# Step sizes of the state-space layer in fp32 from x, four 32-column groups at once, and three small halves made by GpSimd

## The reference

```python
hn = rmsnorm(x, norm_mix_pre[0])                 # x * r(token) * g(feature)
proj = einsum('bsd,de->bse', hn, w_in)           # 1024 -> 2*2048 + 2*8*128 + 32
z, xBC, dt = split(proj, ...)
xBC = silu(causal_dwconv(xBC, conv_w, conv_b))
dt = softplus(dt + dt_bias)                      # 32 step sizes a token, one a head
A_cs = cumsum(dt * A) in chunks of 128 tokens    # decays, used by all 8 groups
```

## Time and profile before

| | |
|---|---|
| median of 3 runs | 1422.06 us (1421.97 to 1422.57) |
| profiled execution, its time | 1422.02 us |
| its span in the trace | 1420.2 us |
| TensorE busy | 1405.7 us, 99% of the span |
| VectorE busy | 1003.5 us, 71% |
| ScalarE busy | 623.9 us, 44% |
| GpSimd busy | 112.3 us, 8% |

### The profile page before, as it was taken

One profiled execution on the slowest core, in us unless ns is written; L12 is line 12 of the kernel. 1 busy time (PEld: TensorE's weight loads), 2 busy tenths in 40 slices (PEclk: granted clock), 3 DMA queues, 4 the chain that ended last, 5 costly groups with the idle time before them and its releaser, 6 DMA issues.

```text
span 1420.2 us, 21794 instructions
## 1 busy us (share of the span) xinstructions
PE 1405.7 (99%) x7550; PEld 1184.2 (83%) x7550; DVE 1003.5 (71%) x1510; ACT 623.9 (44%) x1068; POOL 112.3 (8%) x84
## 2 busy tenths in 40 slices
PE   8999999999999999999999999999999999999997
PEld 7888888888889888888888977778798888888887
DVE  6988888889437888888622676768488888887123
ACT  6666556557344323232322446566653322333221
POOL 0000000000110000000011023232110000000111
PEclk9999999999999999999999999999999999999999
DMA  4443333332231222323324112121312323233331
GB/s 175 171 144 124 144 123 114 135 143 77 90 134 34 101 97 95 102 90 108 108 91 145 38 55 81 60 74 59 112 37 89 104 89 103 90 108 102 102 102 60
DMA packets 37445, 142.34 MB, mean 100 GB/s; under 512 B 4176, under 2 KB 6352, under 8 KB 35344
## 3 DMA queue, kind: packets, MB, share of 16 engines
q1 hardware_dynamic: 37392, 141.63, 29.0%
HBM read 139.38 MB, written 2.23 MB: 100 GB/s over the span
## 4 chain that ended last, share of the span: by engine, by line
PE 94%; DVE 3%; issue 1%; DMA 1%; ACT 1%; SPq 0%; POOL 0%; POOLq 0%; ACTq 0%
PE bank L471 21%; PE bank L473 20%; PE bank L472 20%; PE b_x L471 7%; PE b_x L473 7%; PE b_x L472 7%; PE b_norm L1652 1%; PE b_y L1073 1%; PE b_y L471 1%; PE b_y L472 1%; PE b_y L473 1%; DVE hn_lo L815 1%; PE b_x L1085 1%; PE b_y L1076 1%; DVE mbuf L820 1%
## 5 line engine op out<-in xcount | busy, mean ns | idle before, releaser
L419 ACT ACTIVATE w_hi<-raw 128x1024 fp32r<-128x1024 f32 (+1 forms) x201 | 222.8, 1109 | 401.3 <-PE bank L473 286.4
L434 DVE TENSOR_TENSOR w_lo<-raw,w_hi 128x1024 fp32r<-128x1024 f32 (+1 forms) x181 | 234.1, 1294 | 230.8 <-ACT w_hi L419 230.8
L471 PE MATMUL bank<-hn_hi,w_hi 128*128 128x512 f32 x848 | 337.4, 398 | 1.0 <-DVE hn_lo L796 0.7
L473 PE MATMUL bank<-hn_hi,w_lo 128*128 128x512 f32 x848 | 331.3, 391 | 0.0
L472 PE MATMUL bank<-hn_lo,w_hi 128*128 128x512 f32 x848 | 330.8, 390 | 0.0
L471 PEld LDWEIGHTS bank<-hn_hi,w_hi 128*128 128x128 f32 x848 | 159.6, 188 | 41.8 <-issue 6.4
L473 PEld LDWEIGHTS bank<-hn_hi,w_lo 128*128 128x128 f32 x848 | 159.6, 188 | 34.1
L472 PEld LDWEIGHTS bank<-hn_lo,w_hi 128*128 128x128 f32 x848 | 159.8, 188 | 31.8
L471 PE MATMUL bank<-h_hi,w_hi 128*128 128x512 f32 (+1 forms) x352 | 127.9, 363 | 0.0
L473 PE MATMUL bank<-h_hi,w_lo 128*128 128x512 f32 (+1 forms) x352 | 127.6, 362 | 0.0
L472 PE MATMUL bank<-h_lo,w_hi 128*128 128x512 f32 (+1 forms) x352 | 127.6, 362 | 0.0
(11 more groups left out here) (323 smaller groups left out, 2427.5 us busy)
## 6 DMA issues: line engine op xcount, KB each, us to landing
raw<-w_up SPq DMA_DIRECT2D x80, 512.0 KB, 3.2
raw<-w_mix SPq DMA_DIRECT2D x48, 512.0 KB, 3.3
raw<-w_dn SPq DMA_DIRECT2D x32, 704.0 KB, 4.0
raw<-w_qkv SPq DMA_DIRECT2D x20, 512.0 KB, 3.2
acs_bc<-scratch SPq DMA_DIRECT2D x8, 1024.0 KB, 5.6
ecs_bc<-scratch SPq DMA_DIRECT2D x8, 1024.0 KB, 4.6
raw<-w_sout SPq DMA_DIRECT2D x16, 512.0 KB, 3.2
first_raw<-w_up SPq DMA_DIRECT2D x8, 512.0 KB, 6.3
```

Source lines behind the costliest of these rows:

```text
L419: nc.scalar.activation(halves_of(ph, j if own else rep, own or first and j < 4)[0], raw_of(ph, rep, first and j < 4), ACT.Copy).then_inc(h ...
L434: nc.vector.tensor_tensor(lo, raw_of(ph, rep, first), hi.bitcast(F32), ALU.subtract).then_inc(lo_made, 1)
L471: nc.tensor.matmul(acc[:], wh, hi, start=first, stop=False)
L473: return nc.tensor.matmul(acc[:], wl, hi, start=False, stop=last)
```

## The change

Unit 0 is done anew. Its weights are the 32 real columns only, stored as 128x256, and are multiplied by the gain g once, on VectorE, in place (`raw`). TensorE multiplies them in plain fp32 with x itself (`step_sizes`): chunk 4*part + q writes to the partitions 32q to 32q+31 of one bank, so that four chunks stand in four column groups, in two rounds. What comes out are four partial sums on 128 partitions; the later transposes become products with `stack` (four identity matrices of 32 over each other), which turn and add in one. `d_v` has 128 rows for 32.

Around it the order moves. Unit 1 now runs between the two rounds and behind them; unit 2 starts after chunk 5 of unit 1, and six of its chunks stay behind the norm's sum. ScalarE splits unit 1 after chunk 0 (before: 1), and unit 2 after chunk 3 (before: 7). The low halves of units 2, 4 and 5 are made by GpSimd, not by VectorE. Unit 3 accumulates in another bank, the transposes of `d_v` stand after its first chunk, and there are 8 warm-up matmuls for 10. The load of unit 4's weights waits for the step sizes' product, where it waited for unit 0's low half.

```diff
@@ load_unit
             if ph is MIX and isinstance(j, int) and j == 4:
-                sp.wait_ge(lo_made, 1)
+                sp.wait_ge(unit_done, 1)
@@ warm_up, mix_acc, first_unit
-            for _ in range(10):
+            for _ in range(8):
-            return {2: b_y[:, 0, :], 5: b_y[:, 0, :], 6: b_y[:, 1, :]}.get(j) if j in (2, 5, 6) else acc_of(MIX, j)[:]
+            apart = {2: b_y[:, 0, :], 3: b_x[:, 0, :], 5: b_y[:, 0, :], 6: b_y[:, 1, :]}
+            return apart[j] if j in apart else acc_of(MIX, j)[:]
-            if j in (3, 5, 7):
-                pe.wait_ge(evac["in"], {3: 2, 5: 3, 7: 4}[j])
+            if j in (4, 5, 7):
+                pe.wait_ge(evac["in"], {4: 1, 5: 3, 7: 2}[j])
@@ boundary_pe
-            for j in range(2):
-                pe.wait_ge(lo_made, nxt.U0 + j + 1)
-                for c in range(2):
-                    chunk(j, c)
-            for c in range(2, KC):
-                for j in range(2):
-                    last = chunk(j, c)
-                    if c == KC - 1:
-                        last.then_inc(unit_done, 1)
+            step_sizes(pe, 0)
+            pe.wait_ge(lo_made, 2)
+            chunk(1, 0)
+            chunk(1, 1)
+            step_sizes(pe, 1).then_inc(unit_done, 1)
+            for c in range(2, 5):
+                chunk(1, c)
+            chunk(1, 5)
+            pe.wait_ge(lo_made, 3)
+            chunk(2, 0)
+            chunk(2, 1)
+            chunk(1, 6)
+            chunk(1, 7).then_inc(unit_done, 1)
             pe.wait_ge(sq_added, KC - 1)
             norm_stat(ssq, 0)
-            first_unit(pe, 2, {0: lambda: root_turn(pe, norm_no["pre0"]), 2: lambda: norm_bcast(pe, norm_no["pre0"])})
+            chunk(2, 2)
+            root_turn(pe, norm_no["pre0"])
+            chunk(2, 3)
+            norm_bcast(pe, norm_no["pre0"])
+            for c in range(4, KC):
+                last = chunk(2, c)
+            last.then_inc(unit_done, 1)
+
+        def step_sizes(pe, part):
+
+            pe.wait_ge(lo_made, 1)
+            for q in range(4):
+                c = 4 * part + q
+                pe.wait_ge(x_in_s[c], 16)
+                last = nc.tensor.matmul(bank[0][q * QUAD:(q + 1) * QUAD, :], raw[:, 0, c * QUAD:(c + 1) * QUAD],
+                                        x[:, c, :], start=part == 0, stop=part == 1)
+            return last
@@ boundary_act, in the loop over the chunks m
-                    if m == 1:
+                    if m == 0:
                         split_hi(act, nxt, 1, 1)
-                split_hi(act, nxt, 2, 2)
+                    if m == 3:
+                        split_hi(act, nxt, 2, 2)
@@ boundary_dve
-                    if m == 1:
+                    if m == 0:
                         split_lo_dve(dve, nxt, 1)
-                split_lo_dve(dve, nxt, 2)
                 norm_col(dve, "pre0")
+                dve.wait_ge(lo_made, 3)
                 split_lo_dve(dve, nxt, 3)
@@ first_mix_pe
-            pe.wait_ge(dtv_ready, 1)
-            for c in range(NB):
-                last = nc.tensor.transpose(b_cb[:, c * HS:(c + 1) * HS], d_v[:, c * P:(c + 1) * P], ident[0:HS, 0:HS])
-            last.then_inc(dtv_back, 1)
+            def steps_to_tokens():
+                pe.wait_ge(dtv_ready, 1)
+                pe.wait_ge(stack_made, 5)
+                for c in range(NB):
+                    last = nc.tensor.matmul(b_cb[:, c * HS:(c + 1) * HS], d_v[:, c * P:(c + 1) * P], stack[:],
+                                            start=True, stop=True)
+                last.then_inc(dtv_back, 1)
-            first_unit(pe, 3)
+            first_unit(pe, 3, {0: steps_to_tokens})
@@ dt_dve, mix_dve
-            split_lo_dve(dve, MIX, 4)
-                split_lo_dve(dve, MIX, 5)
@@ block.sync
-            load_unit(sp, MIX, 0, 0)
+            sp.dma_start(raw[:, 0, 0:KC * QUAD], w_mix[0][:, 0:KC * QUAD]).then_inc(raw_in[0], 16)
             sp.dma_start(par[:], params).then_inc(par_in, 16)
             for m in range(KC):
                 sp.dma_start(x[:, m, :], x_in[:, m, :]).then_inc(x_in_s[m], 16)
-                if m == 1:
+                if m == 0:
                     load_unit(sp, MIX, 1, 1)
@@ block.gpsimd, behind the constants
+            pool.wait_ge(hi_made, 3)
+            pool.wait_ge(lo_made, 2)
+            nc.gpsimd.tensor_tensor(own_lo[:], own_raw[:], own_hi[:].bitcast(F32), ALU.subtract).then_inc(lo_made, 1)
             boundary_pool(pool, 0, MIX)
+            for j in (4, 5):
+                pool.wait_ge(hi_made, j + 1)
+                pool.wait_ge(lo_made, j)
+                nc.gpsimd.tensor_tensor(w_lo[:, j % 2, 0:KC * P], raw[:, j % 2, 0:KC * P],
+                                        w_hi[:, j % 2, 0:KC * P].bitcast(F32), ALU.subtract).then_inc(lo_made, 1)
@@ block.scalar
-            split_hi(act, MIX, 0, 0)
+            nc.scalar.activation(spare[:], eps[:], ACT.Copy).then_inc(hi_made, 1)
@@ block.vector
-            split_lo_dve(dve, MIX, 0)
+            raw_landed(dve, MIX, 0, 0)
+            wgt = raw[:, 0, 0:KC * QUAD].rearrange("p (c j) -> p c j", c=KC)
+            nc.vector.tensor_tensor(wgt, wgt, par[:, NORM0:NORM0 + KC].unsqueeze(2).to_broadcast([P, KC, QUAD]),
+                                    ALU.mult).then_inc(lo_made, 1)
             boundary_dve(dve, 0, MIX)
-            dve.wait_ge(unit_done, 1)
-            nc.vector.tensor_tensor(d_v[:], bank[0][0:HS, :], r_pre[0:HS, :], ALU.mult).then_inc(evac["in"], 1)
+            dve.wait_ge(unit_done, 2)
+            nc.vector.tensor_tensor(d_v[:], bank[0][:], r_pre[:], ALU.mult).then_inc(evac["in"], 1)
```

More of the change, by code:

```diff
@@ L137, in trunk @@
         rcol = sb("rcol", [P, NB])
-        sb("lead_norm", [P, 984])
+        stack = sb("stack", [P, QUAD])
+        sb("lead_norm", [P, 952])
         r_pre = sb("r_pre", [P, S])
@@ L169, in trunk @@
             with ExitStack() as lap:
-                d_v = sb("d_v", [HS, S], scope=lap)
+                d_v = sb("d_v", [P, S], scope=lap)
                 d_e = sb("d_e", [HS, S], scope=lap)
@@ L282, in trunk @@
         table_in = sem("table_in")
+        stack_made = sem("stack_made")
         gate_ready, hb_ready, hhi_ready, hlo_ready = (
@@ L653, in chunk @@
                 pe.wait_ge(hnlo_ready, c + 1)
-                return product(acc_of(nxt, j), slot_of(nxt, j), c, hn_hi[:, c, :], hn_lo[:, c, :],
-                               c == 0, c == KC - 1)
-            for j in range(2):
-                pe.wait_ge(lo_made, nxt.U0 + j + 1)
-                for c in range(2):
-                    chunk(j, c)
-            for c in range(2, KC):
-                for j in range(2):
-                    last = chunk(j, c)
-                    if c == KC - 1:
-                        last.then_inc(unit_done, 1)
+                return product(mix_acc(j), slot_of(MIX, j), c, hn_hi[:, c, :], hn_lo[:, c, :], c == 0, c == KC - 1,
+                               halves_of(MIX, j, True))
+            step_sizes(pe, 0)
[11 more added lines that the diff above has]
+            chunk(1, 7).then_inc(unit_done, 1)
             pe.wait_ge(sq_added, KC - 1)
             norm_stat(ssq, 0)
-            first_unit(pe, 2, {0: lambda: root_turn(pe, norm_no["pre0"]), 2: lambda: norm_bcast(pe, norm_no["pre0"])})
+            chunk(2, 2)
[13 more added lines that the diff above has]
+            return last
         def wide_start(pe, b, nxt):
@@ L705, in boundary_act @@
                     nc.scalar.activation(sq_all[:, m, :], x[:, m, :], ACT.Square).then_inc(sq_ready, 1)
-                    if m == 1:
+                    if m == 0:
                         split_hi(act, nxt, 1, 1)
-                split_hi(act, nxt, 2, 2)
+                    if m == 3:
+                        split_hi(act, nxt, 2, 2)
+                act.wait_ge(hi_made, 1)
                 nc.scalar.activation(spare[:], eps[:], ACT.Sqrt).then_inc(table_in, 1)
@@ L1091, in turn_pe @@
             pe.wait_ge(silu_ready, 6 * g + 4)
-            if not first:
+            if first:
+                pe.wait_ge(evac["in"], 4)
+            else:
                 pe.wait_ge(prev_ready, g)
@@ L1390, in mix_dve @@
             if first:
+                dve.wait_ge(lo_made, 6)
                 split_lo_dve(dve, MIX, 6)
@@ L1939, in _ @@
             assert n == N_CONST, n
-            boundary_pool(pool, 0, MIX)
+            nc.gpsimd.memset(stack[:], 0.0).then_inc(stack_made, 1)
+            for q in range(4):
+                pool.wait_ge(stack_made, q + 1)
+                nc.gpsimd.affine_select(out=stack[:], in_=stack[:], compare_op=ALU.not_equal, fill=1.0, base=-q * QUAD,
+                                        pattern=[[-1, QUAD]], channel_multiplier=1).then_inc(stack_made, 1)
+            pool.wait_ge(hi_made, 3)
+            pool.wait_ge(lo_made, 2)
+            nc.gpsimd.tensor_tensor(own_lo[:], own_raw[:], own_hi[:].bitcast(F32), ALU.subtract).then_inc(lo_made, 1)
+            boundary_pool(pool, 0, MIX)
+            for j in (4, 5):
```

(17 more changed lines are left out.)

## The result

| | before | after |
|---|---|---|
| median (lowest to highest) | 1422.06 (1421.97 to 1422.57) | 1429.21 us (1426.36 to 1429.63) |
| profiled execution: time, span | 1422.02, 1420.2 | 1429.21, 1427.4 |
| granted TensorE clock, mean of the span | 0.998 | 0.994 |

The ratio is 1.0043, with a 95% interval of 1.0032 to 1.0055. The forecast was 1425.2 in a range to 1427.0: the direction is right, the size is not, and the median lies above the range.

What follows compares the result with a forecast made beforehand. TensorE, busy 99% of the span, was taken as the bound; `dt_tok`, late through GpSimd's holds on VectorE, makes it stand from 37.6 to 41.7, 3.2 us later than before: 1422.06 becomes 1425.2 us, range 1419.5 to 1427.0.

Steps and rivals of the forecast that it cites:

- the two waits: TensorE's waits at the norm's sum (21.89, TensorE late by 2.1 us) and the turn of `dt_tok` (38.53, slack 0.66 us).
- the signs: Listed trace observations: for the forecast, such as `hn_lo` over 2 us; against it, such as matmuls behind 17 us 0.43 apart.
- The first hold: At chunk 4 of unit 1, GpSimd's low half of unit 2 holds VectorE until 17.05; chunk 4 begins 2.4 us later.
- The norm's sum at 22.4: Behind unit 1's chunk 7, TensorE reaches the norm's sum at 22.4, 0.5 us later than before.
- The later holds: GpSimd's halves of units 4 and 5 delay VectorE by 1.7 us at the first convolution and 2.3 between `t_p` and `dt_tok`.
- The product with `stack` has the width of the transposes: At the product replacing the transposes of `d_v`: same width, so this edit costs nothing.
- TensorE stands until 41.7, where it passed at 38.53: 3.2 us later: At the turn of `dt_tok` (`steps_back`): TensorE arrives at 37.6, waits for `dt_tok` until 41.7, and everything behind shifts 3.2 us.
- Rival 3: TensorE's clock falls in the idle time from 15.6 to 21.6, adding 2.2 us: 1427.4 us; chance 0.11.
- the engine still gets three matmuls every 1.3 us: Argument that TensorE's clock would not fall in the idle time from 15.6 to 21.6, since matmuls keep coming.
- Four column groups: In the step sizes' product the four groups run side by side: 0.9 us a round, 1.8 both, saving 3.7 us.
- Rival 2: No block of VectorE by GpSimd at all: norm's sum at 20.7, `dt_tok` at 36.0, 2.5 us gained, 1419.5; chance 0.15.

Runs made afterwards that it cites:

- the fill at both places: The changed kernel plus idle-filling matmuls, 10 ahead of chunk 4 of unit 1 and 15 ahead of the turn of `dt_tok`; median 1425.36 us, ratio 1.0019.
- e8: The changed kernel with the turn of `dt_tok` moved after chunk 1 of unit 5 and the sums' turn after chunk 0 of unit 6; 1428.91 us, ratio 1.0046.
- e11: The changed kernel with only unit 5's low half back on VectorE, units 2 and 4 staying on GpSimd; 1425.02 us, ratio 1.0018.
- e5: The changed kernel with all low halves on VectorE, unit 2 split after chunk 5, and three unit 2 chunks moved between unit 1's last chunks; 1421.17 us, ratio 0.9989.

## Why the prediction was wrong

- **What bounds the kernel, and the two waits**: right. Both places named decided the time. Of the signs, the three held operations came (2.33, 1.89 and 2.36 us). So did the last one of those that speak against the forecast: matmuls behind 17 us that are 0.43 apart.
- **The first hold**: right. `own_raw` landed at 13.9 (forecast 13.6), GpSimd held until 17.37 (17.05), the last sum of squares ended at 22.3 (22.2).
- **"The norm's sum at 22.4"** failed: 23.79. Of the 1.4 us between, 0.9 are the low clock behind the first wait (5.81 us from chunk 4 to the norm's sum where 4.88 to 4.91 do with the clock up). The rest is that `own_raw` landed 0.3 later than forecast, and that six chunks of TensorE lie between its wait for chunk 4 and the norm's sum (4.1 us of work), which the forecast, going by VectorE alone, didn't add up.
- **The later holds**: right in place and kind, somewhat too large. From the convolution's start to `t_p` the change needs 6.57 us against 5.23 before, 1.34 more where 1.7 was taken; from `t_p` to the end of `dt_tok` 7.07 against 5.01, 2.06 more where 2.3 was taken. Together 3.4 for 4.0, which took 0.6 us off the miss: `dt_tok` was ready at 42.51, 0.8 behind the forecast's 41.7, since `r_pre` came 1.4 late (26.38 for 25.0).
- **"The product with `stack` has the width of the transposes"** was wrong by 0.45 us, which fell into the wait (TensorE came to the turn at 39.55 and waited 3.0 us, where the forecast had 37.6 and some 4): its fp32 product is two passes of 0.11, eight in all, 0.81 us to the next start where the transposes took 0.36.
- **The sum's failed step** is "TensorE stands until 41.7, where it passed at 38.53: 3.2 us later": the sum ends there and puts at nothing what an idle TensorE costs behind its wait. Rival 3 had that for the first idle time only, with a chance of 0.11, and no case had it for the second, the very wait on which the sum rests. There it costs 2.8 us, behind the first 0.9. The waits and holds themselves cost about what the sum says, as the fill at both places shows with 3.04. That this is so near to 3.2 is in part luck: the holds were 0.6 us smaller than taken, and 0.3 us of the 3.04 are the fill running past `dt_tok`. In the change's profile, holds 2.8, the later landing 0.3, the first low stretch 0.9 and the second 2.8 make 6.8 of the 7.15; the remaining 0.4 are open.
- **The argument against rival 3**, "the engine still gets three matmuls every 1.3 us", looked at the wrong stretch. The clock fell at the end of the 2.5 us without any matmul (0.97 over 15.4 to 17.9, 0.50 behind), ahead of those three. The Trainium skill, "TensorE: Matmul & The Clock Gate", Part 1, has the low level as the state of an idle engine: by that rule the trace agrees, with 0.50 behind both idle times, though `e8` and `e11` show 1.00 behind the same first one. With the prices that the change's profile shows, the sum would have been 1425.2 + 2.8 + 0.9 = 1428.9, between its two timings. The prediction weighed it only for the place where it was the smaller cost (2.2 us by rival 3, 0.9 measured, as the clock was back at 21.2).
- **Four column groups**: the second round of `step_sizes` took 12.52 to 13.61, 1.09 us, between the 0.9 taken and the 1.5 estimated from the Trainium skill, "TensorE: Matmul & The Clock Gate", Part 3. The saving was real but fell into the wait, as forecast.
- **Rival 2** (no hold) is out by its own sign: `hn_lo` took 2.33 us, not 0.75. No run has GpSimd's halves without the holds. The nearest to its schedule is `e5` (norm's sum at 20.87 for its 20.7, turn at 36.23 for 36.0), and that is 1.15 us faster than before where rival 2 said 2.5.

## What to carry to other kernels

A wait on TensorE can have two prices: its length, and the matmuls behind it at half clock. Write both into the sum, the second with a chance, wherever waits like these of 2.5 to 3.0 us are forecast; in the change's profile the second price was 3.7 us in all, more than the 3.04 of the holds. GpSimd is no free helper for an operation with two inputs in SBUF while VectorE works on SBUF: each hold here took 1.3 to 2.1 us from VectorE to spare it 1.22. If a wait can't be avoided, first ask what the late engine does next: moving the wait gave nothing, filling it gave back the clock's share, and taking the lateness away gave back all.
